# Joined attention pairs, a norm moved into the feed-forward block, and split pooled and low-rank products, in a two-layer prompt-and-sample step on one NeuronCore

## What is computed

```
proj = h @ w_in                                     # layer 0: 256 Fourier channels, then q, k, v
s_loc = einsum("bqhd,brkhd->bhqrk", qi, kb) * scale + bias      # sample: banded, with a relative bias
s_loc = where(col_ok, s_loc, NEG_INF)
s_ctx = einsum("bqhd,bkhd->bhqk", qi, ck) * scale               # sample: also over cached keys
p = softmax(concatenate([s_loc, s_ctx]))

hp = modulate(xp, norm_mix[1], sh1p, sc1p)          # rmsnorm(x, g) * (1 + scale) + shift
proj = h @ w_in                                     # layer 1
c_out = pool_mix(proj[..., :POOL_CH], pool_w, pool_scale)
zr = centred_shift(proj[..., POOL_CH:], shift_mu)   # x + mu0 * (prev - x) + mu1 * (next - x)
wl, al, gl = low-rank inputs of decay, rate and gate: 384 columns of zr
```

## Time and profile before

| | |
|---|---|
| time, median of 3 runs | 1764.88 us (1762.79 to 1767.28) |
| profiled execution | 1766.47 us, span 1764.4 us |
| mean granted TensorE clock | 0.908 of full |
| busy PE / PEld / DVE / ACT / POOL | 87% / 70% / 65% / 42% / 14% |
| attention, first projection to last output | 74.5 to 300.8 us |
| feed-forward block | 356.7 to 670.1 us |
| norm of layer 1, pooled and low-rank block | 670.4 to 734.2 us |

### The profile page before, as it was taken

One profiled execution on the slowest core, in us unless ns is written; L12 is line 12 of the kernel. 1 busy time (PEld: TensorE's weight loads), 2 busy tenths in 40 slices (PEclk: granted clock), 3 DMA queues, 4 the chain that ended last, 5 costly groups with the idle time before them and its releaser, 6 DMA issues. The chain is left out here.

```text
span 1764.4 us, 33835 instructions
## 1 busy us (share of the span) xinstructions
PE 1530.5 (87%) x13357; PEld 1236.6 (70%) x13357; DVE 1145.3 (65%) x1533; ACT 746.1 (42%) x1133; POOL 255.1 (14%) x276
## 2 busy tenths in 40 slices
PE   4779989799999995789999998977499999999981
PEld 1556666689999993467767767866477888888871
DVE  0157772379877722386777777643487888898874
ACT  2212222353232302153524524323476677788763
POOL 3400000142222120011011011002101110111111
PEclk6888996899999976899999998987699999999996
DMA  8794533078766404021011010015488899999984
GB/s 309 238 316 132 169 123 134 8 223 275 243 217 201 155 1 134 16 63 31 22 41 31 23 40 3 5 62 195 189 320 330 330 379 391 379 370 366 368 312 156
DMA packets 157561, 321.97 MB, mean 182 GB/s; under 512 B 13171, under 2 KB 104645, under 8 KB 151301
## 3 DMA queue, kind: packets, MB, share of 16 engines
q1 hardware_dynamic: 129734, 201.32, 32.0%
q0 software_dynamic: 26416, 114.28, 18.9%
q10 hardware_dynamic: 1296, 4.72, 0.7%
HBM read 299.15 MB, written 24.25 MB: 183 GB/s over the span
## 5 line engine op out<-in xcount | busy, mean ns | idle before, releaser
L2740 DVE TENSOR_TENSOR gate_up_low<-expert_gate_up,gate_up_high 128x1408 fp32r<-128x1408 f32 x147 | 231.6, 1618 | 23.1 <-ACT gate_up_high L2662 23.0
L2662 ACT ACTIVATE gate_up_high<-expert_gate_up 128x1408 fp32r<-128x1408 f32 x147 | 197.8, 1374 | 35.5 <-PE banks L2558 28.6
L2556 PE MATMUL banks<-gate_up_high,gathered_high 128*128 128x512 f32 (+1 forms) x432 | 167.4, 387 | 12.6 <-DVE gate_up_low L2740 12.6
L2558 PE MATMUL banks<-gate_up_high,gathered_low 128*128 128x512 f32 (+1 forms) x432 | 164.6, 381 | 0.0
L2557 PE MATMUL banks<-gate_up_low,gathered_high 128*128 128x512 f32 (+1 forms) x432 | 164.4, 381 | 0.0
L2736 DVE TENSOR_TENSOR down_low<-expert_down,down_high 128x1024 fp32r<-128x1024 f32 x99 | 118.5, 1218 | 52.3 <-ACT down_high L2655 52.1
L2655 ACT ACTIVATE down_high<-expert_down 128x1024 fp32r<-128x1024 f32 x99 | 102.2, 1051 | 76.4 <-PE banks L2558 60.4
L1175 DVE SCALAR_TENSOR_TENSOR mod_sums<-next_mod_w,silu_cond,mod_sums 128x2048 f32<-128x2048 f32 x48 | 125.5, 2660 | 6.3 <-DMA mod_sums<-in_mod_b 6.3
L1051 PE MATMUL banks<-ffn_in_high,gate_up_w_high 128*128 128x384 f32 x352 | 119.0, 338 | 4.3 <-DVE ffn_in_low L1156 4.2
L1052 PE MATMUL banks<-ffn_in_low,gate_up_w_high 128*128 128x384 f32 x352 | 118.7, 337 | 0.0
L1053 PE MATMUL banks<-ffn_in_high,gate_up_w_low 128*128 128x384 f32 x352 | 118.6, 337 | 0.0
(11 more groups left out here) (391 smaller groups left out, 3311.8 us busy)
## 6 DMA issues: line engine op xcount, KB each, us to landing
expert_gate_up<-in_moe_w_up SPq DMA_DIRECT2D x76, 704.0 KB, 7.2
expert_gate_up<-in_moe_w_gate SPq DMA_DIRECT2D x76, 704.0 KB, 7.7
expert_down<-in_moe_w_down POOLq DMA_DIRECT2D x99, 512.0 KB, 5.7
next_mod_w<-in_mod_w POOLq DMA_DIRECT2D x24, 1024.0 KB, 5.2
late_w<-in_mod_w POOLq DMA_DIRECT2D x16, 1024.0 KB, 5.2
gate_up_w<-in_ffn_w_gate SPq DMA_DIRECT2D x22, 512.0 KB, 6.2
gate_up_w<-in_ffn_w_up SPq DMA_DIRECT2D x22, 512.0 KB, 5.6
normed_by_channel<-in_ffn_w_down SPq DMA_DIRECT2D x22, 512.0 KB, 6.4
```

Of the source, the lines that this page charges most:

```text
L2556: nc.tensor.matmul(out, a[0], b[0], start=first, stop=False)
L2558: return nc.tensor.matmul(out, a[1], b[0], start=False, stop=last)
L2662: nc.scalar.activation(WH[:, u % SPLIT, :], raw[:, u % RAW, :], ACT.Copy).then_inc(high, 1)
L2740: v.tensor_tensor(WL[:, u % SPLIT, :], raw[:, u % RAW, :], WH[:, u % SPLIT, :], ALU.subtract).then_inc(low, 1)
```

## The change

Attention: the three loops are written out, and each pair's begin is moved into the pair before. `qT`, `kT`, `V`, `ckT`, the context values and the bias get a second buffer. PE turns the next pair's keys in unit 4 (both into bank 5) and computes its first two scores behind the output products of units 4 and 5. ACT copies the next q behind unit 2 and the next k behind unit 4, and the output of a pair inside the first unit of the next. DVE copies turned keys behind unit 4 and v inside unit 0. The bias addition goes from DVE to POOL. SP requests context keys, values and bias a pair ahead, and the out projection's weights at pair 4. The bias lives in a buffer `front` (640 x 8 floats a partition), which in turn serves as the feed-forward block's raw weights, as the weights of the pooled and low-rank products, and as scratch in the scan.

Feed-forward block: behind the mixer's column products PE turns the normed rows (in `next_mod_w`'s memory), then come the ffn's column products and the gate rows; squares, root, scaling and modulation of `normed(R, 2)` are in ACT's and DVE's lists of this block. SP requests the eleven parameter rows in step 0 and the two weight pieces behind the last split.

`pool_lora`: inputs and weights are split, 120 matmuls replace 40, pooled columns come first, and the shifts stand behind the pooled differences.

```diff
@@ attention
-        qT, kT = sb("qT", [P, TOK]), sb("kT", [P, TOK])
-        V = sb("v", [P, TT, P])
-        ckT = sb("ckT", [P, P])
+        qT, kT = sb("qT", [P, 2, TOK]), sb("kT", [P, 2, TOK])
+        V = sb("v", [P, 2, TT, P])
+        ckT = sb("ckT", [P, 2, P])
+        bias = R.front[:, 0:8 * DEC].rearrange("p (a h t n) -> p a h t n", a=2, h=2, t=2)
...
@@ SyncE
+                sp.wait_ge(pe_done, pe_at("ck.0"))
+                ctx_k_load(R, sp, 1)
+                for j in pairs:
+                    if j < LAST:
+                        if j:
+                            sp.wait_ge(pe_done, pe_at(f"pv5.{j - 1}"))
+                        ctx_v_load(R, sp, j + 1)
+                        bias_loads(sp, j + 1)
+                    sp.wait_ge(dve_done, dve_at(f"v.{j}"))
+                    store(sp, j)
+                    if j + 2 < PAIRS:
+                        for m in range(3):
+                            sp.wait_ge(projected, proj_at("qkv"[m], j + 1))
+                            if m == 2:
+                                sp.wait_ge(pe_done, pe_at(f"ck.{j + 1}"))
+                                ctx_k_load(R, sp, j + 2)
+                            qkv_load(R, sp, m, j + 2)
+                    if j == LAST - 1:
+                        ahead(sp)
@@ GpSimd
-                for u in range(EARLY_SUMS // 4 + 2, 2 * KT):
-                    late_load(R, pool, u)
+                sums = list(range(EARLY_SUMS // 4 + 2, 2 * KT))
+                pool.wait_ge(win, 16)
+                for j in pairs:
+                    pool.wait_ge(b_loaded[j % 2], 16 * (j // 2) + 16)
+                    flat = bias[:, j % 2, :, :, :].rearrange("p h t (r k) -> p (h t r) k", k=GRID_W)
+                    nc.gpsimd.tensor_tensor(flat, flat, window[:, :].unsqueeze(1).broadcast_to([P, 16, GRID_W]), ALU.add).then_inc(windowed, 1)
+                    for u in sums[3 * j:3 * j + 3]:
+                        late_load(R, pool, u)
@@ TensorE
-                    pe.wait_ge(act_done, act_at("out", j))
-
-                with pe.Fori(0, PAIRS - 1) as j:
-                    turn(j, True)
-                turn(PAIRS - 1, False)
+                turned_keys(0)
+                scores(0, 0)
+                scores(1, 0)
+                for j in pairs:
+                    for u in range(6):
...
+                        weighed(u, j)
...
+                        if u == 4 and j < LAST:
+                            turned_keys(j + 1)
+                        valued(u, j)
                         if u + 2 < 6:
-                            scores(u + 2)
+                            scores(u + 2, j)
+                        elif j < LAST:
+                            scores(u - 4, j + 1)
@@ VectorE
+                def turned_keys(j):
+                    dve.wait_ge(pe_done, pe_at(f"kp.{j}"))
+                    if j:
+                        dve.wait_ge(stored, 32 * j)
+                    nc.vector.tensor_copy(ckT[:, j % 2, :], R.B[5][:, 0:P]).then_inc(dve_done, dve_inc(f"ck.{j}"))
+                    nc.vector.tensor_copy(kp[:, :], R.B[5][:, P:2 * P]).then_inc(dve_done, dve_inc(f"kp.{j}"))
...
-                    dve.wait_ge(pe_done, pe_at("pv5", j))
-                    dve.wait_ge(stored, 32 * j + 32)
+                        scored(u, j)
+                        next_sum()
+                        if u == 0:
+                            dve.wait_ge(projected, proj_at("v", j))
...
+                        weighed(u, j)
+                        next_sum()
+                        if u == 4 and j < LAST:
+                            turned_keys(j + 1)
@@ dense_ffn, SyncE
+                    if f == 0:
+                        scan_row_loads(R, sp)
+
+                sp.wait_ge(low, 2 * NF)
+                front_loads(R, sp)
@@ dense_ffn, TensorE
+                columns(0)
+                pe.wait_ge(scaled, 3)
+                pe.wait_ge(gated, 6)
+                for k in range(KT):
+                    if k == KT - 1:
+                        pe.wait_ge(ht_even, 1)
+                    for t in range(TT):
+                        mm = nc.tensor.transpose(R.B[turn_bank[k]][:, t * P:(t + 1) * P], XN[:, t, k * P:(k + 1) * P], R.ident[:, :])
+                    mm.then_inc(turned, 1)
+                pe.wait_ge(R.mod_columns, 1)
+                columns(1)
@@ layer1
-        normed(R, 2)
@@ pool_lora, TensorE
-                for n, m in enumerate((2, 3, 4, 0, 1)):
...
-                        mm = nc.tensor.matmul(R.B[n][:, 0:TOK], W[:, k, m * P:(m + 1) * P], R.HT[:, k, :], start=(k == 0), stop=(k == KT - 1))
+                for n in range(5):
+                    s, out = n % FRONT_SPLIT, R.B[n][:, 0:TOK]
+                    pe.wait_ge(w_low, n + 1)
                     for k in range(KT):
+                        if n == 0:
+                            pe.wait_ge(in_low, k + 1)
+                        nc.tensor.matmul(out, WH[:, s, k, :], HH[:, k, :], start=(k == 0), stop=False)
+                        nc.tensor.matmul(out, WH[:, s, k, :], HL[:, k, :], start=False, stop=False)
+                        mm = nc.tensor.matmul(out, WL[:, s, k, :], HH[:, k, :], start=False, stop=(k == KT - 1))
@@ pool_lora, ScalarE
+                for n in range(5):
+                    if n + FRONT_SPLIT < 5:
+                        split_w(n + FRONT_SPLIT)
+                    projected(n)
+                    if n >= 3:
+                        act.wait_ge(dve_done, dve_at(f"z{n - 1}"))
+                        nc.scalar.activation(R.lora[:, (2, 0)[n - 3], :], z[:, n - 3, :], (ACT.Sigmoid, ACT.Tanh)[n - 3])
@@ pool_lora, VectorE
+                split_w(2)
+                split_w(3)
+                dve.wait_ge(act_done, act_at("m1"))
...
+                    if wd == 4:
+                        split_w(4)
...
+                for n in (2, 3, 4):
+                    shifted(n)
```

537 lines of the change are left out of this document (317 added, 220 removed).

## The result

The changed kernel takes 1717.93 us (median of 4 runs, 1717.3 to 1718.27) against 1763.84 (4 runs, 1762.53 to 1767.28): a ratio of 0.9736, 95% interval 0.972 to 0.9753. The forecast was 1721.0. In a second measurement, with 5 runs of it and 9 of the kernel before, it took 1715.32 (1711.95 to 1721.03), ratio 0.9718 (0.9694 to 0.9741); so a median is known to some 3 us. The profiled execution took 1718.27 us, its span is 1716.6, 47.8 less than before; the working had 44.1.

The account below looks back on a forecast made before the run. TensorE was taken to bound the attention inside pairs, serial chains the pair edges and the stretch up to the scan. Savings of 18.8 + 8.6 + 16.7 = 44.1 us gave 1721 us (1715 to 1727 at 0.62; range 1706 to 1737).

Parts of the forecast that it names:

- Attention: Attention stage: joined pairs gain 17.9 us, pair 0 loses 1.75, the last edge gains 2.7; 18.8 us saved in all.
- first term: Inside an attention pair: six units of TensorE work without a stall take 26.8 us.
- The first stall: Before unit 5's probabilities: VectorE waits for turned keys with that unit's scores behind; TensorE stalls 1.0 us, bounds 0 and 2.
- the second stall: Window addition on GpSimd disturbs VectorE: 1.8 us lost there a pair (0 to 2.4), of which 0.9 reaches TensorE.
- pair 0: First attention pair: longer by 1.75 us, for the turned keys, the score product and the stall before unit 5.
- the last edge: From the last output product to the first column product: 4.4 us becomes 1.7, a gain of 2.7.
- Norm: End of the feed-forward block: norm moved beside the column products, 7.6 us plus 1 for the clock; 8.6 saved, 5.5 to 11.5.
- Pooled and low-rank block: Block before the scan: early rows and weights with split products, 50.8 us becomes 34.1; 16.7 saved, bounds 11 and 19.
- DVE's pace: Rival, attention: VectorE sets the pace, a pair takes 31.2 us, 10 us less gain, 1731 us; chance 0.18.
- No stall: Rival, attention: pairs run at TensorE's 26.8 us without stalls, 1712 us; chance 0.12.
- Pairs that don't join: Rival, attention: late stores and bias keep each edge as long as now, attention gains nothing, 1740 us; chance 0.05.
- the half clock: Rival, attention: stalls leave TensorE at the half clock, 26.8 us become some 50 a pair, 1806 us; chance 0.03.

Follow-up runs that it names:

- run 5: The kernel before with the changed attention alone, norm and pooled and low-rank block as before: 1748.72 us, ratio 0.9903.
- run 3: The changed kernel with the window addition back on VectorE and the turned keys copied behind unit 5's scaled probabilities: 1704.54 us, ratio 0.9653.
- run 1: The changed kernel with the bias-plus-window addition moved from GpSimd back to VectorE, behind unit 4's last late sum: 1708.3 us, ratio 0.9687.
- run 7: The changed kernel with GpSimd's 20 writes of zero rows moved behind the late weight loads, four a pair: 1713.43 us, ratio 0.97.
- Run 2: The changed kernel with VectorE's copies of turned keys moved behind unit 5's scaled probabilities, window addition still on GpSimd: 1706.26 us, ratio 0.967.
- run 9: The changed kernel itself measured once more, unedited: 1715.32 us, ratio 0.9718.
- run 10: The changed kernel with window addition on VectorE, turned keys copied behind unit 5, zero rows later, and gate rows among one-column products: 1695.6 us, ratio 0.9609.
- run 11: The changed kernel with window addition on VectorE, turned keys copied behind unit 5, zero rows later, and plain pooled and low-rank products: 1684.0 us, ratio 0.9532.
- run 4: The changed kernel with the norm's 24 turned blocks behind both halves of the column products, not between them: 1721.26 us, ratio 0.9747.
- Run 6: The changed kernel with 40 plain float32 products and no splits in the pooled and low-rank block, early weights and order kept: 1704.44 us, ratio 0.966.
- run 12: The changed kernel with window addition on VectorE, keys copied behind unit 5, zero rows later, gate rows among column products, plain pooled and low-rank products: 1683.93 us.

## Why the prediction was right, and where it was not

**Attention, 18.8 forecast, 16.7 measured** (run 5 by the medians, and the table with its later start of 2.1 us; without that start the table has 18.7). The mechanism, PE's own work plus two stalls on DVE, was right, and its first term exact: 26.8 us of work a pair, where run 3 has 26.75. The first stall (1.0 forecast) shows as 0.67 and costs 0.9 (27.64 in run 1 less 26.75 in run 3). **The term that was mis-sized is the second stall**: 1.8 us lost on DVE of which 0.9 reach PE. DVE loses 2.57, and 1.55 reach PE (29.19 less 27.64). I took the loss from DVE's addition of 2.60 us and POOL's of 2.52, as if the two had disturbed each other. Their surroundings in the trace of before show that another addition of POOL's is what DVE met:

```profile
765.83 1.81 POOL L1603 TENSOR_TENSOR log_sum<-k_mod,decay_after 128x768 f32<-128x768 f32 x1 [31.12 <-ACT states L1925]
765.85 2.60 DVE L2105 TENSOR_TENSOR beta<-neg_kk_a,growth 128x768 f32<-128x768 f32 x1
767.60 2.52 POOL L1604 TENSOR_TENSOR log_decay<-neg_kk_a,decay_after 128x768 f32<-128x768 f32 x1
```

So 1.65 us of DVE were lost to an addition of 1.81, nearly the whole of it, which the row alone did not tell. In the attention, too, DVE's instruction stands for as long as POOL's runs. The Trainium skill, "Trainium Architecture — The Big Picture", What this means for kernel authors, calls the port pair of DVE and GpSimd an exclusive lock and not a split of bandwidth; the traces agree, with 3.85 us instead of 1.28 beside an addition of 2.36, and 4.00 instead of 0.29 beside one of 2.81 (of which 0.9 us isn't explained, run 7). By that rule alone the DVE loss would have been 2.4.

A second miss is that I added the two stalls. Run 2 shows that one slack served both: DVE's wait of 3.2 us for turned keys (forecast; 2.91 measured) is what made POOL's disturbance visible. Third, pair 4: POOL has 14 late loads for five pairs, three a pair but only two in pair 4, so the last pair's window addition (230.29) falls into its middle beside a sum of 3.30 us. The order of POOL's list shows that, and I hadn't counted it: 1.66 us. Together the pairs gained 14.2 us where 17.9 was forecast.

Against these, pair 0 (-1.75 forecast, -1.7 measured) and the last edge (2.7 and 2.73) were right, and the last pair gained 3.5 that I did not have: from its first column product to its first gate row are 6.00 us instead of 9.22, and its first 16 instructions take 1.95 instead of 3.57, since PE now comes to them without idle time and at the full clock. I had counted the edge's idle time, and not what it cost behind. The size of the 3.5 is uncertain, as this stretch differs by up to 3 us between profiles with the same attention (runs 9 to 11). That the attention's sum fits is luck: this gain, which I had not priced, made up for the 3.7 us that the pairs fell short. The later start of 2.1 us is variation.

**Norm, 8.6 forecast, 11.9 measured** (bounds 5.5 to 11.5). Starting the turned blocks 9.7 us in was right to 0.5 (9.18). The clock that they give back was taken as 1 us between bounds of 0 and 4; run 4 shows 3.3 in the column products. With that and half a microsecond each from the earlier start and the gate rows (9.03 us instead of 9.5) the part ends a little beyond its upper bound.

**Pooled and low-rank block, 16.7 forecast, 18.6 to the scan's first projection.** First piece at 10.5 (10.2 measured), 4.2 a piece (4.1), pooled differences done at 26.5 (26.4), the shifts 5.4 us instead of 4.82. The end came 1.5 us sooner than 34.1, because ACT's two pooled copies lie under the last shift and not behind it. So the forecast for this block was good; what it did not ask is whether the split earns anything. It took the split and the early weights as one. Run 6 separates them: rows, weights and order bring all of it, the split takes at least 5.9 us back. The row for it was there: 28.8 us for 40 plain products at a clock of 0.90 is 26 at the full clock, no more than the forecast's 27.3 us for piece 4, with nothing on DVE.

**Rivals.** DVE's pace (pairs of 31.2) did not come, though its mechanism did, with the larger loss. No stall (1712) is what runs 2 and 3 make. Pairs that don't join and the half clock are excluded by 29.19 us and a granted clock of 1.00 in pairs 1 to 4. The scan and the expert stage were held unchanged: 0.4 us.

## What to carry to other kernels

Work handed from VectorE to GpSimd isn't off VectorE if the two run at the same time: here 2.36 us there cost 2.57, twice what the same addition costs on VectorE (1.22), which had a wait to hide it. Before two small stalls are added up, ask whether one slack pays for both; moving a copy that waits behind the work that doesn't was worth as much as removing the disturbance. And a change that bundles an early load with a cheaper product should be priced with each alone: the split of the products shortened TensorE's work by 5 us and lengthened the chain that ended the block.

## What the runs showed of the hardware that I had not expected

- A VectorE instruction that meets a GpSimd addition stands at least until that is done, whatever its own length. The scalings of 0.29 us end within 0.1 us of it, after 4.00 and 2.18 us (run 7). Late sums of 1.28 us end 1.09 us behind it, whether they start 0.4 us ahead of it (3.85 us, changed kernel) or 0.15 us behind its start (3.30 us, pair 4).
- 24 turned blocks that themselves run at the half clock (5.14 us at 0.50) are followed by some 3 to 4 us at the full clock (0.84 over 4.96 us); a gate row behind every 16 instructions of one-column products changes nothing that runs 10 and 12 could show.
- The first DMA request of ScalarE in the expert stage takes 2.8 to 4.7 us in the kernel before, the changed one and every run with split products or with the pooled and low-rank block of before, and 0.40 in the three with plain products and the new order (6, 11 and 12). Behind the long one PE waits 3 to 4 us (3.08 in the changed kernel, 3.95 in run 9). The kernel before has plain products too, so these are not the cause by themselves; it is left open. The durations (ns) of the nine requests, in the changed kernel and in run 6:

```profile
L2891 ACTq DMA_DIRECT2D expert_rows<-normed_by_channel x9: 338/338/3076, 1310.9 to 1682.6; - x9
```

```profile
L2873 ACTq DMA_DIRECT2D expert_rows<-normed_by_channel x9: 338/338/403, 1299.0 to 1667.5; - x9
```
